# A fifth seven-product couple in each wide pair of the down projection, with the plain evictions on ScalarE

## The reference, cut to what matters

```python
f = jnp.square(jax.nn.relu(rms_norm(x, g_ffn_pre) @ w_up)) @ w_down   # x 256x2048, w_up 2048x8192, w_down 8192x2048
return x + rms_norm(f, g_ffn_post)
```

## Time and profile before

| | before |
|---|---|
| median of 3 runs | 1889.64 us (1889.15 to 1889.72) |
| profiled execution | 1889.38 us |
| its span in the trace | 1887.3 us |
| PE busy | 1874.9 us, 99% |
| DVE busy | 1497.9 us, 79% |
| ACT busy | 1111.4 us, 59% |

### The profile page before, as it was taken

One profiled execution on the slowest core, in us unless ns is written; L12 is line 12 of the kernel. 1 busy time (PEld: TensorE's weight loads), 2 busy tenths in 40 slices (PEclk: granted clock), 3 DMA queues, 4 the chain that ended last, 5 costly groups with the idle time before them and its releaser, 6 DMA issues.

```text
span 1887.3 us, 27369 instructions
## 1 busy us (share of the span) xinstructions
PE 1874.9 (99%) x9950; PEld 1672.1 (89%) x9950; DVE 1497.9 (79%) x1885; ACT 1111.4 (59%) x1485; POOL 118.5 (6%) x166
## 2 busy tenths in 40 slices
PE   9999999999999999999999999999999999999998
PEld 7988988988988998898888888889889889989987
DVE  6886657898699689788877757678977996897886
ACT  6455656855665565566554556568556655645662
POOL 3920010000000000000000000100000000000000
PEclk9999999999999999999999999999999999999999
DMA  8665366757566666767576554586676666567673
GB/s 290 201 221 181 112 201 226 236 182 255 189 198 216 214 198 195 236 202 241 210 234 225 187 168 134 170 275 194 197 236 207 195 212 221 183 207 235 221 257 124
DMA packets 170068, 390.92 MB, mean 207 GB/s; under 512 B 12161, under 2 KB 14321, under 8 KB 168433
## 3 DMA queue, kind: packets, MB, share of 16 engines
q1 hardware_dynamic: 167904, 377.58, 61.8%
q10 hardware_dynamic: 2064, 12.08, 1.7%
HBM read 382.53 MB, written 7.08 MB: 206 GB/s over the span
## 4 chain that ended last, share of the span: by engine, by line
PE 95%; DVE 3%; issue 1%; ACT 0%; DMA 0%; POOL 0%; DVEq 0%; POOLq 0%; ACTq 0%
PE acc_pair L573 25%; PE acc_pair L578 13%; PE acc_pair L539 8%; PE acc_pair L540 8%; PE acc_pair L541 8%; PE acc_pair L874 7%; PE acc_pair L873 7%; PE acc_pair L872 7%; DVE w_lo L1445 1%; PE t_bank L874 1%; PE t_bank L873 1%; PE t_bank L872 1%; PE o_bank L791 1%; DVE h_both L1501 1%; PE ssa_bank L872 1%
## 5 line engine op out<-in xcount | busy, mean ns | idle before, releaser
L995 ACT CAST w_hi<-raw 128x1024 fp32r<-128x1024 f32 x687 | 703.6, 1048 | 476.4 <-DVE raw L1998 190.7
L1445 DVE TENSOR_TENSOR w_lo<-raw,w_hi 128x1024 fp32r<-128x1024 f32 x687 | 827.4, 1232 | 169.0 <-ACT w_hi L995 161.8
L573 PE MATMUL acc_pair<-h_both,w_hi 128*128 128x512 f32 x2176 | 560.3, 380 | 0.2
L573 PEld LDWEIGHTS acc_pair<-h_both,w_hi 128*128 128x128 f32 x2176 | 371.4, 190 | 30.4 <-issue 0.5
L578 PEld LDWEIGHTS acc_pair<-h_both,w_lo 128*128 128x128 f32 x2176 | 327.4, 190 | 29.2
L578 PE MATMUL acc_pair<-h_both,w_lo 128*128 128x256 f32 x2176 | 330.5, 274 | 0.0
L872 PE MATMUL acc_pair<-w_hi,f_hi 128*128 128x512 f32 x504 | 191.0, 379 | 0.0
L873 PE MATMUL acc_pair<-w_lo,f_hi 128*128 128x512 f32 x504 | 191.0, 379 | 0.0
L874 PE MATMUL acc_pair<-w_hi,f_lo 128*128 128x512 f32 x504 | 191.0, 379 | 0.0
L539 PE MATMUL acc_pair<-w_hi,h_both 128*128 128x512 f32 x444 | 170.4, 384 | 1.8 <-DVE w_lo L1445 1.6
L540 PE MATMUL acc_pair<-w_lo,h_both 128*128 128x512 f32 x444 | 168.3, 379 | 0.0
(11 more groups left out here) (252 smaller groups left out, 2293.8 us busy)
## 6 DMA issues: line engine op xcount, KB each, us to landing
raw<-in_w_up SPq DMA_DIRECT2D x256, 512.0 KB, 4.4
raw<-in_w_down SPq DMA_DIRECT2D x240, 512.0 KB, 5.0
raw<-in_w_in SPq DMA_DIRECT2D x128, 512.0 KB, 4.7
raw<-in_w_out SPq DMA_DIRECT2D x64, 512.0 KB, 5.3
raw_side<-in_w_down SPq DMA_DIRECT2D x16, 512.0 KB, 7.0
x_kept<-x ACTq DMA_DIRECT2D x4, 1024.0 KB, 6.2
x<-x_kept ACTq DMA_DIRECT2D x4, 1024.0 KB, 6.1
x<-in_x SPq DMA_DIRECT2D x8, 256.0 KB, 7.5
```

The costliest lines, as they stand in the source:

```text
L573: pe.matmul(acc_pair[b][:, m, :], w_hi[:, slot, col:col + P], x_both.rearrange("p s (a n) -> p s n a", a=2), start=(slot, k) == (0, 0), st ...
L995: act.copy(w_hi[:, half * PAIRS + p, :], raw[:, p, :]).then_inc(hi_made, 1)
L1445: dve.tensor_tensor(w_lo[:, slot, :], src[:, p, :], w_hi[:, slot, :].bitcast(F32), ALU.subtract).then_inc(lo_made, 1)
```

## The change

Each wide pair gets a fifth seven couple, and the order of ks differs between the two pairs of a group. `q` = 0 has its seven couples at places 0, 4, 6, 10, 12 and ends with a plain couple; `q` = 1 has them at 0, 4, 8, 12, 14 and ends with a seven couple. The activation sums of the fifth couple are made in the last unit of the up projection. Evictions that need no addition (the shared sums of groups 0 and 1, the output banks of group 0) are done by ACT (`first_shared`, `first_sums`); before, DVE did them all. The small tables of the rotary angles share memory with the new sums.

```diff
-SEVEN_AT = (0, PAIRS, RING, RING + PAIRS)
-SEVEN_UNIT = ((1, 0), (1, 1), (2, 0), (2, 1))
-K_ORDER = (4, 5, 0, 1, 6, 7, 2, 3, 8, 9, 12, 13, 10, 11, 14, 15)
+SEVEN_AT = ((0, 4, 6, 10, 12), (0, 4, 8, 12, 14))
+COUPLES = len(SEVEN_AT[0])
+SEVEN_UNIT = ((1, 0), (1, 1), (2, 0), (2, 1), (3, 0))
+PLAIN_K = (0, 1, 2, 3, 14, 15)
+def t_buffer(q, n):
+    return (q * COUPLES + n) % 2
...
+                def two_hi(g, q, i):
+                    hu = hu0 + HU_F + g * HU_GROUP + 2 * CHUNKS + PAIR_HALVES * q + i // PAIRS
+                    if i in SEVEN_AT[q]:
+                        act.wait_ge(t_third, seven_no(l, g, q, SEVEN_AT[q].index(i)) + 1)
+                    split_hi(hu, i // PAIRS % 2, (i % PAIRS, i % PAIRS + 1))
+                def first_shared(g):
+                    if g == 0:
+                        act.wait_ge(x_saved, 16 * T * (l + 1))
+                    act.wait_ge(t_used, 3 * seven_no(l, g, 0, COUPLES) - 1)
+                    for k, bank in enumerate((ssa_bank, t_bank[0], t_bank[1], o_bank)):
+                        act.copy(kept_sums[:, 1 - pair_at(g, 0), k, :], bank[:, :]
+                                 ).then_inc(shared_free, 1)
+                def first_sums(q):
...
+                            act.mul(dst, put_back(acc_pair[t][:, c, :]),
+                                    rstd[:, COL_X2 + t:COL_X2 + t + 1]).then_inc(acc_free[t], 1)
...
                     if not last:
-                        for n in range(PAIR_HALVES):
-                            seven_hi(g, 1, n, hu + 12 + n, n % 2)
-                        split_hi(hu + 16, 0)
+                        wide_hi(g, 1, 0, 2)
+                        if g < T:
+                            first_shared(g)
+                        two_hi(g, 1, 2)
+                        if first:
+                            first_sums(0)
+                        wide_hi(g, 1, 4)
+                        split_hi(hu + 16, 0, (0, 1))
+                        if first:
+                            first_sums(1)
+                        split_hi(hu + 16, 0, (2, 3))
                         split_hi(hu + 17, 1)
...
+                def wide_lo(g, q, begin):
+                    for i in range(begin, SLOTS, 2):
+                        if i in SEVEN_AT[q]:
+                            weight_sums(g, q, SEVEN_AT[q].index(i))
+                        two_lo(g, q, i)
+                        if i in SEVEN_AT[q]:
+                            sums_lo(g, q, SEVEN_AT[q].index(i))
...
                 def wide_pair(g, q, first, last=False):
...
-                    seven_lo(g, q, 2, hu + 2, 0)
-                    seven_lo(g, q, 3, hu + 3, 1)
+                    wide_lo(g, q, (6, 4)[q])
                     if q == 0 and not last:
-                        weight_sums(g, 1, 0, nxt)
-                        split_lo(nxt, 0, (0, 1))
+                        weight_sums(g, 1, 0)
+                        two_lo(g, 1, 0)
                         sums_lo(g, 1, 0)
-                        shared_sums(g)
-                        split_lo(nxt, 0, (2, 3))
-                        wide_sums(g, q, first)
-                        seven_lo(g, 1, 1, nxt + 1, 1)
+                        if g >= T:
+                            shared_sums(g)
+                        two_lo(g, 1, 2)
+                        if not first:
+                            wide_sums(g, q)
...
                     def last_unit():
...
-                        seven_lo(g, 0, 0, nxt, 0)
+                        weight_sums(g, 0, 0)
+                        two_lo(g, 0, 0)
+                        sums_lo(g, 0, 0)
+                        two_lo(g, 0, 2)
                         s_rest(g, 3)
                         turned_sum(g, u, 0)
-                        weight_sums(g, 0, 1, nxt + 1)
+                        weight_sums(g, 0, 1)
                         f_stands(g, u, 0)
+                        s_sums(g, 4)
                         turned_lo(g, u, 0)
-                        split_lo(nxt + 1, 1, (0, 1))
+                        two_lo(g, 0, 4)
                         turned_sum(g, u, 1)
-                        split_lo(nxt + 1, 1, (2, 3))
                         f_stands(g, u, 1)
                         turned_lo(g, u, 1)
+                        s_rest(g, 4)
                         sums_lo(g, 0, 1)
```

More of the change, by code:

```diff
@@ L137, with k_order @@
 WIDE_LAYER = 2 * FF_GROUPS - 1
-SEVEN_AT = (0, PAIRS, RING, RING + PAIRS)
-SEVEN_UNIT = ((1, 0), (1, 1), (2, 0), (2, 1))
-K_ORDER = (4, 5, 0, 1, 6, 7, 2, 3, 8, 9, 12, 13, 10, 11, 14, 15)
+SEVEN_AT = ((0, 4, 6, 10, 12), (0, 4, 8, 12, 14))
+COUPLES = len(SEVEN_AT[0])
+SEVEN_UNIT = ((1, 0), (1, 1), (2, 0), (2, 1), (3, 0))
+PLAIN_K = (0, 1, 2, 3, 14, 15)
 SHARED = 4
+def k_order(q):
+    plain, order = iter(PLAIN_K), []
+    for i in range(0, SLOTS, 2):
+        if i in SEVEN_AT[q]:
+            u, b = SEVEN_UNIT[SEVEN_AT[q].index(i)]
+            order += [4 * u + 2 * b, 4 * u + 2 * b + 1]
+        else:
+            order += [next(plain), next(plain)]
+    return order
+K_ORDER = (k_order(0), k_order(1))
+def t_buffer(q, n):
+    return (q * COUPLES + n) % 2
 def pair_at(g, q):
@@ L880, in seven @@
                 def seven(g, q, n, hu, result):
-                    i = SEVEN_AT[n]
+                    i = SEVEN_AT[q][n]
                     no, s0, s1 = seven_no(l, g, q, n), i % RING, i % RING + 1
-                    k0, k1 = K_ORDER[i], K_ORDER[i + 1]
+                    k0, k1 = K_ORDER[q][i], K_ORDER[q][i + 1]
                     first = n == 0
-                    begin, end = first and (q == 1 or g == 0), n == len(SEVEN_AT) - 1 and q == 0
+                    begin, end = first and (q == 1 or g == 0), n == COUPLES - 1 and q == 0
+                    closing = i == SLOTS - 2
                     left, right = c_cols(0), c_cols(1)
@@ L912, in seven @@
                         bank_free(0, 0, q, result)
-                    three(acc_pair[0][:, 0, :], f_hi[:, k1, early], f_lo[:, k1, early],
-                          w_hi[:, s1, left], w_lo[:, s1, left], first, False)
+                    mm = three(acc_pair[0][:, 0, :], f_hi[:, k1, early], f_lo[:, k1, early],
+                               w_hi[:, s1, left], w_lo[:, s1, left], first, closing)
+                    if closing:
+                        mm.then_inc(acc_done, 2)
                     if first:
@@ L943, in down_wide @@
                                            f_lo[:, kt, h_cols(t)], w_hi[:, slot, c_cols(c)],
-                                           w_lo[:, slot, c_cols(c)], begin, i == SLOTS - 1)
+                                           w_lo[:, slot, c_cols(c)], begin,
+                                           i == SLOTS - 1 or i == last_plain and (t, c) == (1, 1))
                                 if (t, c) == (1, 1):
@@ new lines, in wide_hi @@
+                def wide_hi(g, q, begin, end=SLOTS):
+                    for i in range(begin, end, 2):
+                        two_hi(g, q, i)
+                        if i in SEVEN_AT[q]:
+                            sums_hi(g, q, SEVEN_AT[q].index(i))
+                def first_shared(g):
[5 more added lines that the diff above has]
+                                 ).then_inc(shared_free, 1)
@@ new lines, in first_sums @@
+                def first_sums(q):
+                    result = a0 + ACC_F + CHUNKS + 2 * q
+                    hu = hu0 + HU_F + 2 * CHUNKS + PAIR_HALVES * q
+                    act.wait_ge(rstd_ready, T + l * RS_LAYER + RS_X2 + T)
+                    for t in range(T):
+                        for c in range(2):
+                            if q == 0 and t == 0:
+                                act.wait_ge(acc_done, result + c + 1)
+                            elif q == 0 and c == 0:
+                                act.wait_ge(third_done, wide_done(l, 0))
+                            elif q == 0 or (t, c) == (0, 1):
+                                act.wait_ge(w_used, RING + PAIRS * (hu + PAIR_HALVES))
+                            elif t == 0:
+                                act.wait_ge(acc_done, result + 2)
+                            elif c == 0:
+                                act.wait_ge(t_used, 3 * seven_no(l, 0, q, COUPLES))
+                            dst = halves(acc[:, t, c_cols(2 * pair_at(0, q) + c)])
+                            act.mul(dst, put_back(acc_pair[t][:, c, :]),
+                                    rstd[:, COL_X2 + t:COL_X2 + t + 1]).then_inc(acc_free[t], 1)
@@ L2091, in wide_pair @@
                     else:
-                        split_lo(nxt, 0)
-                        wide_sums(g, q, first)
+                        split_lo(nxt, 0, (0, 1))
+                        if not first:
+                            wide_sums(g, q)
+                        split_lo(nxt, 0, (2, 3))
                         split_lo(nxt + 1, 1)
```

166 lines of the change are left out of this document (80 added, 86 removed).

## The result

The changed kernel takes 1930.28 us (median of 4 runs, 1928.86 to 1931.38), the kernel before 1889.42 (4 runs, 1889.15 to 1889.72): a ratio of 1.0216, 95% interval 1.0198 to 1.0233. It is 41 us slower; that it is slower is clear, whether by more or less than 2% is not, since the interval holds both. The profiled execution took 1929.72 us, its span 1927.5.

What follows compares the result with a forecast made beforehand. PE's stream bounds the kernel before; with the change DVE's queue becomes the bound of the wide stage. Groups lose 2.7, 5.0, 6.1 and 4.7: 18.5 us a layer, 37 for two; 1889.4 + 37 = 1926 us, range 1905 to 1938.

Steps and rivals of the forecast that it cites:

- DVE's chain: DVE's work in the wide pairs as one queue that PE waits for; the fifth couple adds 4.20 us per pair.
- The saving: PE in the 14 wide pairs: 42 matmuls fewer at 0.2158 us from start to start, 9.1 us in all.
- The head of the chain: Group 2, start of `q` = 0: DVE's steps come net 0.7 us later, weight sums beginning at 9.22.
- The second wait: Group 2, between `q` = 0 and `q` = 1: PE waits 3.8 us for DVE's shared sums, landing at 43.5.
- The first wait: Group 2, `q` = 0, place 12: splits land at 30.07, PE wants them at 28.49, a wait of 1.6 us.
- The waits in `q` = 1: Group 2, second pair: PE waits 0.4 us for an output bank, 1.2 at place 14, 0.7 at the end.
- The load waits: DVE's waits for `raw` tiles: five per group at 0.75 us on its chain; without any, the time falls to 1905.
- the clock falls: Rival: at each of four long waits one couple runs at 1.2 GHz; some 13 us more, 1939; 15%.
- A sign of being wrong: Granted clock below 1.00 in the middle; the other sign was PE beginning `q` = 1 of group 2 within 40 us.
- The lead covers it: Rival: DVE's added work falls into its idle time, only the 9.1 us saved show; 1880 us; 5%.
- Half of it: Rival: load waits vanish and the late start does not happen, so PE's waits go or shrink; 1905 us; 15%.
- ACT is the new bound: Rival, groups 0 and 1: evictions cost ACT twice what was taken, 6 us more, 1932 us; 7%.

## Why the prediction was right, point by point

**The direction and the time.** 1926 was forecast, 1930.28 measured, within the range. The cause is the one named: 4.20 us more on DVE's chain per pair against 0.65 saved on PE. The room of "some 3 to 4 us" that the prediction read for DVE was 2.7 and 4.3 us in the two pairs; the working did not rest on it but on the chain. The experiments that take one part each show it: the load on DVE without the couple costs 47 us where the change costs 41, the matmuls left out without that load save, the evictions alone do nothing.

**The saving.** 0.2158 us per matmul, 9.1 us: shown by the kernel with the matmuls left out and the output sums early (9.0).

**The head of the chain.** Forecast: `t_lo` at about 7.55 after the pair's start, the weight sums at 9.22. Measured 7.65 and 9.32 (715.77 and 717.44 less 708.12).

**The second wait.** Forecast 3.8 us in group 2, the shared sums landing at 43.5. They landed at 751.33, 43.2 after the start; the wait is 3.47 us in the first layer and 2.81 in the second. In groups 0 and 1 forecast 1.5 for ACT's copies, measured 0.4 to 1.3. In group 3 forecast 3.7, measured 3.30 and 2.97; the wait listed there is the one for the output sums, which the prediction had behind the shared sums in the same chain.

**The first wait.** Forecast 1.6 us, measured 1.0 at 737.96 and up to 1.7 elsewhere.

**The waits in `q` = 1.** Forecast for group 2: 0.4 for an output bank, 1.2 at place 14 and 0.7 at the end. None of the three came in either layer. In group 1 the bank's wait of 1.4 came with 1.15 and 1.14, the end's 0.7 with 0.56, and the one at place 14 with nothing in the first layer and 0.37 in the second.

**The load waits.** The prediction put five of 0.75 us on the chain of a group, 3.75 us. DVE's timeline has 0.7, 0.9, 1.5 and 0.6 us for the four groups of the first layer and 1.4, 3.2, 1.6 and 0.3 for those of the second, single ones from 0.18 to 0.76 and one of 1.96. This term was too large. What the groups cost:

| per layer | forecast | layer 1 | layer 2 |
|---|---|---|---|
| group 0 | +2.7 | +2.2 | +3.1 |
| group 1 | +5.0 | +3.8 | +6.0 |
| group 2 | +6.1 | +5.3 | +5.8 |
| group 3 | +4.7 | +4.6 | +4.0 |
| sum | 18.5 | 15.9 | 18.9 |

The layers differ most in group 1: PE's waits there are 0.8, 1.7, 0.9, 1.1, 0.4 and 0.6 us in the second layer and 1.1, 0.7, 1.2 and 0.6 in the first. In DVE's timeline one wait for a load has grown, at the weight sums of the fourth seven couple, here first in group 1 of the first layer and then in the second:

```profile
561.81 0.69 DVE L2077 TENSOR_TENSOR raw<-raw 128x512 f32<-128x512 f32 x1 [0.28 <-DMA raw<-in_w_down]
...
1518.81 0.69 DVE L2077 TENSOR_TENSOR raw<-raw 128x512 f32<-128x512 f32 x1 [1.96 <-DMA raw<-in_w_down]
```

The load waits of the two layers differ by 2.9 us in all (3.6 and 6.5), their losses by 3.0; by group the two differences run together too (0.7, 2.3, 0.2, -0.3 for the waits, 0.9, 2.2, 0.5, -0.6 for the losses). So a late load reaches PE in full in this execution, as one chain would have it. Why that load was late was not found.

**What the sum left out.** The wide stages cost 34.8 us where 37 were forecast. The other 5.4 us: 0.8 ahead of group 0, and 4.6 behind the stages. These last are the rival "the clock falls", which had 15%. It came true beside the forecast, not in its place, and was oversized: 13 us were worked out, and four stretches at 1.2 GHz cost 8.1. In the narrow units of the first layer 918.78 to 924.91 are 14 distances in 6.13 us instead of 3.02, in those of the second 1875.87 to 1880.67 are 14 in 4.80. In group 2 the slow matmuls of the first layer (751.39 to 754.41) take 3.02 us for 7 distances instead of 1.51, those of the second (1710.01 to 1713.41) 3.40 for 8 instead of 1.73. The rival's text had half of the cost in group 2 hidden behind further waits of PE for DVE. No wait follows there in that pair; whether the slow matmuls stand in the place of the forecast's 0.4, 1.2 and 0.7 us is not shown.

**A sign of being wrong that came.** The prediction called itself wrong if the granted clock fell below 1.00 in the middle, and it did, four times. The chain and its waits stood the test, the assumption that a wait costs only itself did not. The forecast's waits of PE come to 46.1 us (37, and the 9.1 saved beside them); those that the trace lists in the wide stages come to 32.6 (the six rows shown, and 1.1 for output sums at the end of group 1), about 36 with 0.16 us more for each of the 24 as worked out in the last section. So it was in part luck that the time landed so near: waits and load waits that were too large and a clock that was left out offset each other.

**The rivals that fell.** "The lead covers it" needed the shared sums before 38.2 after the start; they came at 43.3. "Half of it" had the load waits vanish and no late start; the head of the chain is 0.8 us later than before (7.65 against 6.85), and DVE's load waits, though smaller than taken, add up to 10.1 us. "ACT is the new bound" falls with the kernel of the couples alone: without the evictions on ACT the time is 11 us longer, and PE's waits for ACT's copies are 3.3 us in all, less than the forecast's 1.5 at each of four boundaries.

## What to carry to other kernels

An engine that is 79% busy over the program can be full in the one stage that a change touches: add its work and its idle time up over that stage, and follow its queue from the place where its lead is built, before trading another engine's instructions for its own. A microsecond at the head of such a chain counts in full, so small steps belong into the gaps in which the engine waits anyway (9.5 us for a move of four small instructions in each group). And an idle engine is no free one: offload to POOL only what does not keep DVE out.

## What the runs showed of the hardware

- A subtraction of 128x1536 float32 values takes POOL 3.45 to 4.02 us in the rows above and DVE 1.75; a `raw` difference or a split of DVE that starts during it ends only after it (0.69 us becomes 3.94, two splits of 2.35 become 4.77).
- The granted clock fell after a shorter idle time than at the program's end, where PE was idle from 1879.05 and the clock still 1.00 until 1882.00. In the kernel with the matmuls left out PE was idle for 2.08 us before 1711.86, started again at full clock, and was at 1.2 GHz in the middle of the work that followed:

```profile
1710.00:1712.00 2.00, 0.14 (x1) 0.15 (x2) 2.00 (x4) 1.26 (x2) 0.00 (x0) 1.00 0.75 212
1712.00:1714.00 2.00, 2.00 (x10) 1.80 (x11) 2.00 (x3) 0.27 (x1) 0.00 (x0) 0.75 0.79 227
1714.00:1716.00 2.00, 2.00 (x8) 1.73 (x7) 2.00 (x3) 1.72 (x2) 0.00 (x0) 0.50 0.60 153
1716.00:1718.00 2.00, 2.00 (x13) 1.80 (x12) 1.63 (x2) 0.38 (x1) 0.00 (x0) 0.90 0.91 325
```

- A longer wait need not be followed by a fall. In the kernel with the couples alone PE was idle for 3.04 us before 589.85, and the clock stayed at 1.00 from 590 to 620. Which waits bring one is open.
- In the two kernels with the shared sums first all of PE's waits in the wide pairs are 1.7 us or shorter, and the mean clock is 0.999, as in the kernel before.
- A wait costs PE somewhat more than the idle time listed. Before 905.53 it is 1.40 us, but from the start of the last matmul, 903.75, to the next it is 1.78, which is 1.56 more than a distance of 0.2158.
- At 1.2 GHz a matmul of 512 columns stands 0.427 us from the next, at 2.4 GHz 0.2158.
